# Two-layer encoder step on one core: FFN norm by single tiles, scalars and rows of ones moved, RWKV state chain begun earlier

## What is computed

```python
def _layer(x, past, mem_k, mem_v, l, mw, ow):
    y, new_state = _mixer_sublayer(_rmsnorm(x, norm_mix_pre), past, l, mw)
    x = x + _rmsnorm(y, norm_mix_post)
    x = x + _rmsnorm(_cross_attention(_rmsnorm(x, norm_x_pre), mem_k, mem_v, w_xq, w_xo), norm_x_post)
    x = x + _rmsnorm(_swiglu(_rmsnorm(x, norm_ffn_pre), w_ffn_in, w_ffn_out), norm_ffn_post)
...
    # in the mixer: one projection for all three branches
    a_q, a_k, a_v, a_f, b_q, b_k, b_v, c_in, gate_in = _split_cols(h @ w_in, IN_SPLITS)
    # the scalar of differential attention
    lam = jnp.exp(jnp.sum(lq1 * lk1)) - jnp.exp(jnp.sum(lq2 * lk2)) + lam_init
...
def step(S, xs):  # RWKV-7, frame by frame
    rt, wt, kt, vt, kkt, at = xs
    sa = jnp.einsum('bhvk,bhk->bhv', S, -kkt)
    S = S * wt[:, :, None, :] + sa[..., None] * (kkt * at)[:, :, None, :] + vt[..., None] * kt[:, :, None, :]
    return S, jnp.einsum('bhvk,bhk->bhv', S, rt)
```

## Time and profile before

| what | value |
|---|---|
| runs | 3005.76, 3007.36, 15319.49 us; median 3007.36 us |
| profiled execution | 3008.48 us, its span 3006.7 us |
| TensorE busy | 2861.5 us, 95% |
| weight loads of TensorE | 2644.9 us, 88% |
| VectorE busy | 1637.3 us, 54% |
| ScalarE busy | 746.2 us, 25% |
| transfers | 290.26 MB, 97 GB/s on average |
| chain that ended last | 81% TensorE, 9% VectorE, 3% ScalarE, 2% transfers |

### The profile page before, as it was taken

The page is one execution under the profiler, slowest core; times in us unless marked ns, Lnnn a source line. Parts: engine busy times, 40 slices in busy tenths (PEclk is TensorE's granted clock), DMA queues, the critical chain, the costliest instruction groups (busy, mean ns, idle before and its releaser), DMA issues.

```text
span 3006.7 us, 63127 instructions
## 1 busy us (share of the span) xinstructions
PE 2861.5 (95%) x26468; PEld 2644.9 (88%) x26468; DVE 1637.3 (54%) x3027; ACT 746.2 (25%) x1789; POOL 243.6 (8%) x423
## 2 busy tenths in 40 slices
PE   7999999999999989999989999999999999899998
PEld 6877788999999789999988777799999997899998
DVE  4444554666674356664364445546666633566633
ACT  1133333323233330000112333342222323200001
POOL 1111111000000100000001211120000000000000
PEclk9999999999999999999989998899999999999999
DMA  4443345222163223332224434362222531233331
GB/s 123 125 131 99 98 130 138 83 79 73 39 185 98 60 80 89 87 88 86 78 78 134 114 96 121 98 161 72 78 62 65 175 98 43 85 88 88 87 86 62
DMA packets 420762, 290.26 MB, mean 97 GB/s; under 512 B 38544, under 2 KB 386352, under 8 KB 420352
## 3 DMA queue, kind: packets, MB, share of 16 engines
q1 hardware_dynamic: 398496, 228.64, 27.3%
q0 software_dynamic: 21984, 57.59, 6.0%
HBM read 232.12 MB, written 54.07 MB: 95 GB/s over the span
## 4 chain that ended last, share of the span: by engine, by line
PE 81%; DVE 9%; ACT 3%; DVEq 3%; issue 2%; DMA 2%; ACTq 0%; SPq 0%
PE PS L714 33%; PE PS L781 10%; PE PS L1077 7%; PE PS L1019 7%; PE PS L692 4%; PE PS L946 2%; PE PS L1226 2%; DMA U<-gate_scratch 2%; ACT U L1333 1%; PE PS L657 1%; PE PS L1056 1%; PE PS L863 1%; PE PS L828 1%; ACT U L1336 1%; PE PS L730 1%
## 5 line engine op out<-in xcount | busy, mean ns | idle before, releaser
L714 PE MATMUL PS<-U_r,WHI 128*128 128x272 f32 x2656 | 475.4, 290 | 18.0 <-DVEq L1833 9.2
L1336 ACT COPY U<-PS 128x272 f32<-128x272 f32 (+9 forms) x756 | 263.3, 372 | 752.4 <-PE PS L1077 140.0
L1822 DVE CAST WHI<-ring 128x1024 fp32r<-128x1024 f32 (+1 forms) x240 | 164.2, 684 | 512.4 <-PE PS L714 379.2
L714 PEld LDWEIGHTS PS<-U_r,WHI 128*128 128x128 f32 x2656 | 387.2, 189 | 23.3 <-DVEq L2250 10.8
L714 PE MATMUL PS<-brT_r,WHI 128*128 128x272 f32 x1728 | 357.5, 288 | 0.0
L714 PE MATMUL PS<-U_r,WLO 128*128 128x272 f32 x1696 | 351.2, 289 | 0.0
L714 PE MATMUL PS<-hT_r,WHI 128*128 128x272 f32 x1696 | 351.1, 289 | 0.0
L1832 DVE TENSOR_TENSOR WLO<-ring,WHI 128x1024 fp32r<-128x1024 f32 (+1 forms) x240 | 289.8, 1208 | 19.0 <-issue 0.9
L781 PE MATMUL PS<-U_r,WHI 128*128 128x272 f32 x832 | 268.2, 322 | 15.8 <-ACT U L1336 15.7
L714 PE MATMUL PS<-brT_r,WLO 128*128 128x272 f32 x1344 | 278.2, 288 | 0.0
L714 PEld LDWEIGHTS PS<-brT_r,WHI 128*128 128x128 f32 x1728 | 271.7, 188 | 0.2
(11 more groups left out here) (328 smaller groups left out, 4470.6 us busy)
## 6 DMA issues: line engine op xcount, KB each, us to landing
ring<-in_w_in_dram SPq DMA_DIRECT2D x126, 512.0 KB, 4.2
ring<-in_w_ffn_in_dram SPq DMA_DIRECT2D x88, 512.0 KB, 3.8
ring<-in_w_ffn_out_dram SPq DMA_DIRECT2D x32, 448.0 KB, 3.7
proj_scratch<-U POOLq DMA_DIRECT2D x104, 136.0 KB, 2.0
U<-proj_scratch SPq DMA_DIRECT2D x48, 272.0 KB, 4.4
ring<-in_w_branch_dram SPq DMA_DIRECT2D x48, 256.0 KB, 3.3
gate_scratch<-U POOLq DMA_DIRECT2D x88, 136.0 KB, 3.1
U<-gate_scratch SPq DMA_DIRECT2D x44, 272.0 KB, 2.9
```

The costliest lines, as they stand in the source:

```text
L714: ins = mm(PS[:, 2 * q + h, 0:HT], w, half(x, h), start=(first and k == 0 and n == 0), stop=(last and k == kn - 1 and n == len(terms) - 1))
L1336: return act.copy(out, in_)
L1822: copy(hi, src)
```

## The change

- FFN norm: x is updated, split and multiplied one tile at a time, not two. VectorE's `updated(b)` scales and adds one tile, `low(b)` follows with one tile and its own `x_split`; ScalarE makes one high part and one square in turn; TensorE takes 12 matmuls of one input tile, then its 4 sum matmuls. `X_SPLITS` counts eight signals in place of four.
- Input projection: the lambda scalars, ScalarE's exponential between them and the rows of ones move behind the split and copy of the second output tile (v = 1).
- RWKV: the turn of the sample's starting state moves on TensorE from behind stage 10 to behind the second sum ahead of the stages, its copy on VectorE ahead of stage 1. VectorE evacuates only group 0 of stage 10 before the chain; groups 1 and 2 come behind the first and the second decay multiply, and `rw_free` behind them.
- Forgetting attention: the second weight split of a pass moves from step 8 to step 9.

```diff
@@ -52,7 +52,7 @@
-X_SPLITS = 4 + 6 + 4
+X_SPLITS = 4 + 6 + 8
...
@@ -719,10 +719,11 @@
 
                 pe.wait_ge(split_done, l * SPLITS + v + 1 + 2)
                 freed(l, g + 1)
-                for k0 in range(0, KM, 2):
-                    pe.wait_ge(x_split, l * X_SPLITS + need + k0 // 2 + 1)
+                step = 2 if sums is None else 1
+                for k0 in range(0, KM, step):
+                    pe.wait_ge(x_split, l * X_SPLITS + need + k0 // step + 1)
                     for j in range(2):
-                        for k in (k0, k0 + 1):
+                        for k in range(k0, k0 + step):
                             whi, wlo = (w[:, (v + j) % 2, k, :] for w in (WHI, WLO))
                             xhi, xlo = rhs(k)
                             for n, (w, x) in enumerate(((whi, xhi), (whi, xlo), (wlo, xhi))):
@@ -732,8 +733,7 @@
                         if k == KM - 1:
                             ins.then_inc(tile_done, 1)
                     if sums is not None:
-                        for a in (k0, k0 + 1):
-                            norm_sum(l, sums, a)
+                        norm_sum(l, sums, k0)
...
@@ -1065,6 +1065,11 @@
                         gate(q0 + 1, 1, it=it)
                         pe.wait_ge(rw_in, g * 2 + 2)
                         sums(W_RAW[:, 2, :]).then_inc(rw_sum, 1)
+                        halves = (slice(0, 64), slice(64, 128))
+                        eye = const("stack")[:, 0:64]
+                        for r in halves:
+                            ins = mm(PS[r, 5, 256:320], ST[r, 11, :], eye[r], start=True, stop=True)
+                        ins.then_inc(rw_state, 1)
                         both(q0 + 2, it)
...
@@ -1146,11 +1151,6 @@
-                        halves = (slice(0, 64), slice(64, 128))
-                        eye = const("stack")[:, 0:64]
-                        for r in halves:
-                            ins = mm(PS[r, 5, 256:320], ST[r, 11, :], eye[r], start=True, stop=True)
-                        ins.then_inc(rw_state, 1)
                         for c in range(9):
...
@@ -1385,9 +1385,6 @@
-                act.wait_ge(lam_step, l * 2 + 1)
-                f(small[:, 14:16], small[:, 12:14], ACT.Exp)
-                act.drain().then_inc(lam_step, 1)
...
@@ -1404,6 +1401,10 @@
                     tile(l, G_IN + v)
                     copy(half(EST[:, e % 4, :], 0), PS[:, 2 * IN_PAIR[v], 0:HT]).then_inc(tile_freed_act, 1)
+                    if v == 1:
+                        act.wait_ge(lam_step, l * 2 + 1)
+                        f(small[:, 14:16], small[:, 12:14], ACT.Exp)
+                        act.drain().then_inc(lam_step, 1)
                     e += 1
...
@@ -1715,12 +1716,10 @@
-                for a in range(0, KM, 2):
-                    for b in (a, a + 1):
-                        act.wait_ge(x_updated, l * 24 + 16 + b + 1)
-                        f(HF[:, b, :], xT[:, b, :], ACT.Copy, scale=vec("norm_ffn_pre", b)).then_inc(h_ready, 1)
-                    for b in (a, a + 1):
-                        norm_square(l, 4, b)
+                for b in range(KM):
+                    act.wait_ge(x_updated, l * 24 + 16 + b + 1)
+                    f(HF[:, b, :], xT[:, b, :], ACT.Copy, scale=vec("norm_ffn_pre", b)).then_inc(h_ready, 1)
+                    norm_square(l, 4, b)
                 norm_rstd(l, 4, RSF)
...
@@ -1849,24 +1848,6 @@
-                dve.wait_ge(vec_loaded, (l + 1) * 16 * 19)
-                tt(lamp[:, :, :], lam4[:, 0:4:2, :], lam4[:, 1:4:2, :], ALU.mult)
-                dve.drain()
-                dve.tensor_reduce(small[:, 12:14], lamp[:, :, :], AX.X, ALU.add)
-                dve.drain().then_inc(lam_step, 1)
-                dve.wait_ge(lam_step, l * 2 + 2)
-                c0 = _c["lam"][0]
-                tt(small[:, 16:17], small[:, 15:16], small[:, 14:15], ALU.subtract)
-                dve.drain()
-                tt(small[:, 16:17], small[:, 16:17], CB[:, ds(l + c0, 1)], ALU.subtract)
-                tt(small[:, 17:18], vec("diff_subln", 0), CB[:, ds(l + (c0 + 2), 1)], ALU.mult)
-                dve.drain()
-                dve.memset(FQ[0][64:66, :, :], 1.0)
-                dve.memset(FK[0][64:66, :, :], 1.0)
-                dve.memset(ONES, 1.0)
-                dve.drain().then_inc(fx_rows, 1)
...
@@ -1881,6 +1862,23 @@
+                    if v == 1:
+                        dve.wait_ge(vec_loaded, (l + 1) * 16 * 19)
+                        tt(lamp[:, :, :], lam4[:, 0:4:2, :], lam4[:, 1:4:2, :], ALU.mult)
+                        dve.drain()
+                        dve.tensor_reduce(small[:, 12:14], lamp[:, :, :], AX.X, ALU.add)
+                        dve.drain().then_inc(lam_step, 1)
+                        dve.wait_ge(lam_step, l * 2 + 2)
...
+                        dve.drain()
+                        dve.memset(FQ[0][64:66, :, :], 1.0)
+                        dve.memset(FK[0][64:66, :, :], 1.0)
+                        dve.memset(ONES, 1.0)
+                        dve.drain().then_inc(fx_rows, 1)
...
@@ -1948,8 +1946,8 @@
-                        if k in (3, 8):
-                            late_split(3 * it + k // 8)
+                        if k in (3, 9):
+                            late_split(3 * it + k // 9)
...
@@ -2144,6 +2142,8 @@
+                        dve.wait_ge(rw_state, g * 10 + 1)
+                        copy(ST[:, 8, :], PS[:, 5, 256:320]).then_inc(rw_chain, 1)
                         dve.drain()
                         for gr in range(3):
                             dve.sem_inc(rw_ev[gr], 1)
...
@@ -2199,18 +2199,19 @@
-                        for s in range(1, 11):
+                        for s in range(1, 10):
                             for gr in range(3):
                                 evac(s, gr)
-
-                        dve.wait_ge(rw_state, g * 10 + 1)
-                        copy(ST[:, 8, :], PS[:, 5, 256:320]).then_inc(rw_chain, 1)
-                        dve.drain().then_inc(rw_free, 1)
+                        evac(10, 0)
                         for c in range(9):
                             dve.wait_ge(rw_state, g * 10 + c + 2)
                             to = c + 1 if c < 7 else c + 2
                             ts(ST[:, to, :], PS[:, 2 * (c // 3) + c % 3 % 2, 0:CHUNK], DCOL[:, c:c + 1], None, ALU.mult) \
                                 .then_inc(rw_chain, 1)
+                            if c < 2:
+                                evac(10, c + 1)
+                            if c == 1:
+                                dve.drain().then_inc(rw_free, 1)
                             if c % 3 == 2:
                                 evac(11, c // 3)
                         dve.sem_inc(rp_y, 1)
...
@@ -2326,28 +2327,23 @@
-                def scaled(a):
-                    for b in (a, a + 1):
-                        stt(hT[:, b, :], hT[:, b, :], vec("norm_x_post", b), RS, ALU.mult, ALU.mult)
+                def updated(b):
+                    stt(hT[:, b, :], hT[:, b, :], vec("norm_x_post", b), RS, ALU.mult, ALU.mult)
                     dve.drain()
-
-                def added(a):
-                    for b in (a, a + 1):
-                        tt(xT[:, b, :], xT[:, b, :], hT[:, b, :], ALU.add).then_inc(x_updated, 1)
-
-                def low(a):
-                    for b in (a, a + 1):
-                        dve.wait_ge(h_ready, l * 24 + 16 + b + 1)
-                        stt(hTR[:, b, :], xT[:, b, :], vec("norm_ffn_pre", b), HF[:, b, :].bitcast(F32), ALU.mult, ALU.subtract)
+                    tt(xT[:, b, :], xT[:, b, :], hT[:, b, :], ALU.add).then_inc(x_updated, 1)
+
+                def low(b):
+                    dve.wait_ge(h_ready, l * 24 + 16 + b + 1)
+                    stt(hTR[:, b, :], xT[:, b, :], vec("norm_ffn_pre", b), HF[:, b, :].bitcast(F32), ALU.mult, ALU.subtract)
                     dve.drain().then_inc(x_split, 1)
 
-                scaled(0)
-                added(0)
-                for a in range(2, KM, 2):
-                    scaled(a)
-                    low(a - 2)
-                    added(a)
+                updated(0)
+                updated(1)
+                for b in range(2, KM):
+                    low(b - 2)
+                    updated(b)
                 low(KM - 2)
+                low(KM - 1)
                 dve.wait_ge(xa_stored, (l + 1) * 32)
```

More of the change, by code:

```diff
@@ L1883, in _ @@
                     e += 1
+                    if v == 1:
[5 more added lines that the diff above has]
+                        dve.wait_ge(lam_step, l * 2 + 2)
+                        c0 = _c["lam"][0]
+                        tt(small[:, 16:17], small[:, 15:16], small[:, 14:15], ALU.subtract)
+                        dve.drain()
+                        tt(small[:, 16:17], small[:, 16:17], CB[:, ds(l + c0, 1)], ALU.subtract)
+                        tt(small[:, 17:18], vec("diff_subln", 0), CB[:, ds(l + (c0 + 2), 1)], ALU.mult)
+                        dve.drain()
```

(4 more changed lines are left out.)

## The result

The changed kernel took 2967.3 us, the median of four executions, against 3009.2 us for the kernel before, also four in the same series. That is 42 us less, where 26.6 were forecast, and 8 us under the range of 2975 to 2990. One execution of each kernel was a slow one (6009.5 and 15319.5 us); over the other three the medians are 2962.6 (2959.4 to 2972.0) and 3007.4 us, 45 us apart, with a ratio of 0.9853, 95% interval 0.9827 to 0.9878. Two later series of the same changed kernel gave 2981.1 and 2981.0 us.

The account below looks back on a forecast made before the run. TensorE was taken to bound the kernel. Terms 12.8 (scalars) + 0.9 (FFN) + 6.2 (RWKV) + 6.7 (forgetting attention) = 26.6 us, so 3008.5 - 26.6 = 2981.9 us; range 2975 to 2990.

Parts of the forecast that it names:

- scalars: holes: Input projection: third tile's weight split no longer waits behind scalars and rows of ones; TensorE starts 4.07 and 3.76 us sooner, 7.8.
- scalars: clock behind the hole: Input projection: the 112 matmuls behind the shortened hole run at full clock, 2.33 + 2.70 = 5.0 us saved; other bound 0.
- FFN norm: FFN norm by single tiles: first matmul 2.02 us sooner, 0.46 left per layer, 0.9 in all; bounds 4.0 to -4.6.
- RWKV, eight passes: RWKV state chain: third product's last term 0.89 us sooner, less 0.12, 0.77 x 8 = 6.2 us; bounds 0 and 8.5.
- split in the forgetting attention: Forgetting attention: weight split moved a step later ends TensorE's 1.12 us hole in six passes, 6.7 us; bounds 0 and 7.4.
- The first rival: Input projection: the short hole behind the second tile keeps the half clock, 5.0 us not had, 2986.9 us; chance 0.08.
- the wait before the third tile: FFN norm: TensorE waits about 0.8 us before the third FFN tile, whose weights are split when tile 0 is done.
- the return to the norm's sums: FFN norm: sums interleaved eight times, not four; each return costs TensorE 0.20 us, four more of them 0.8.
- the 0.12 for the moved turning matmuls: RWKV: the 4 turning matmuls, moved into a stretch that TensorE bounds, cost 576.52 - 576.40 = 0.12 us.
- RWKV gives nothing: RWKV: evacuations between the first steps hold the chain as before, kernel at 2988.1 us; chance 0.10.

Follow-up runs that it names:

- the four filled runs: 12 weight-split matmuls moved between sample transposes and values in differential attention: kernel before 2981.2 us; changed kernel 2958.1, 2960.1, and 2957.5 with ten extra norm-sum matmuls.
- the filled changed kernel: Changed kernel with 12 weight-split matmuls moved between the differential attention's 32-wide sample transposes and values: 2958.1 us, then 2960.1 against 2981.0 unaltered.

## Why the prediction was wrong

Term by term, in the two profiled executions:

| step | forecast | measured |
|---|---|---|
| scalars: holes | 7.8 | 3.74 + 3.89 = 7.6 |
| scalars: clock behind the hole | 5.0 | 2.06 + 2.43 = 4.5 |
| FFN norm | 0.9 | 0.47 + 0.62 = 1.1 |
| RWKV, eight passes | 6.2 | 8 x 0.47 = 3.8 |
| split in the forgetting attention | 6.7 | 3.7 + 0.8 = 4.5 |
| differential attention | none | 13.8 + 10.7 = 24.5 |
| all else | none | -0.2 |

**The scalars: right.** In the first layer the hole went to 1.02 and not to 0.7, since from the split's start to TensorE's it took longer than the 2.08 forecast: 50.67 - 48.18 = 2.49. In the second layer it was 2.07 and the hole 0.60. The first rival, that a short hole keeps the half clock, fell: clock 1.00 in the window that begins with the third tile. The rule of the Trainium skill that was weighed (TensorE: Matmul & The Clock Gate, section A second HAM failure mode: psum-queue depth-cycling) speaks of frequent micro-idles, and this was one isolated hole: the clock stayed at 1.00 behind it, and 4.5 of the 5.0 us came.

**The FFN norm: right in mechanism and in size.** The first tile came 2.1 us sooner relative to the norm (forecast 2.02) and the wait before the third tile is 0.51 (forecast about 0.8). The term that was a little too dear is the return to the norm's sums: a tile with its sums takes TensorE 2.42 us at full clock (sums at 1071.98, 1074.41 and 1076.82), where 2.52 were forecast.

**RWKV: one term mis-sized.** The chain gained what was forecast: from its first product to the last term of the third 555.25 - 553.53 = 1.72 us, against 2.66 before, 0.94 for a forecast of 0.89. What failed is the 0.12 for the moved turning matmuls. It was read off the start times of one engine where they stood behind 64-wide work of their kind. Between the sums (L1056) and the stages they stand between 128-wide matmuls. TensorE's timeline from the sums to the first stage, of before and then of after:

```profile
609.44 1.13 PE L1056 MATMUL PS<-U,CB 128*128 128x288 f32 x4
...
616.54 4.49 PE L1077 MATMUL PS<-U 64*64 64x128 f32 x84
```
```profile
585.63 1.13 PE L1056 MATMUL PS<-U,CB 128*128 128x288 f32 x4
586.70 0.33 PE L1071 MATMUL PS<-CB,U 64*64 64x64 f32 x4
...
593.16 4.50 PE L1082 MATMUL PS<-U 64*64 64x128 f32 x84
```

616.54 - 609.44 = 7.10 became 593.16 - 585.63 = 7.53. They cost 0.43 (0.43 to 0.47 in the eight passes), 3.5 times the forecast, and 0.94 - 0.43 is the 0.5 of a pass. The rival "RWKV gives nothing" is wrong too.

**The weight split: right, and given back.** Six passes are 1.18 shorter each, 7.1 us, a little over the 6.7. But the second layer's first pass is 2.8 us longer, at half clock (window of after):

```profile
1583.40:1590.20 6.80, 6.38 (x27) 5.98 (x27) 1.07 (x4) 1.69 (x6) 3.15 (x5) 0.50 0.28 78
```

**The step that failed** is none of the four. The sum took the clock of every stage that the change doesn't touch as given: a term put at nothing without a reason, which measured 24.5 us in the differential attention of the two profiled executions. The prediction asked "does this hole still cost the clock?" in one place, and its range of 15 us had no term for the clock anywhere else. Yet the profiled kernel before spends 127 us of its span at half clock, worth 63 us, which is more than the whole change; the changed one spends 69. Over all 13 executions of the changed kernel: full-clock time 2925.8 on average, 17.9 under before, against 26.6 - 5.0 = 21.6 forecast. Of the 3.7 missing some 2 are the way that a hole in half-clock time counts (an estimate from where the half clock lies in the trace of before); RWKV's 2.4 less and what the FFN and the split gave more make up the rest. Half-clock time is 59 to 119 and on average 99, some 30 less than before, worth 15 us, where the forecast had 5. So the change saves about 33 us on average, 18 of work and waiting and 15 of clock, and 23 to 50 against the average of before in a given execution. That the median of the 13, 2980.0, is near the 2981.9 forecast is partly luck, two errors that cancel: 3.7 us too much from the work, 10 too little from the clock.

**What is shown and what is not.** Shown: the time that the sum missed is half-clock time in stages that the change leaves as they were. A delay of 0.9 to 2.7 us in an unchanged kernel moves its time by -18 to +6 us, through half-clock time. With 12 matmuls put into the thin stretch both kernels have less half-clock time in their own series, 75 for 125 and 67 for 108 us. Supported but not shown: that the thin stretch is what makes the clock fall. For it, the half-clock time is only 41 to 84 us in every execution of the four filled runs, of both kernels. Against it as the only cause, filling shifts the later work too, a delay alone did as much once, and the first layer's first pass still fell in all three traces of the filled changed kernel. Not shown: why the change lowers the half-clock time on average. It shifts the first attention by 10 us and the second by 33, and nothing here says that another 33 would have done as well; the delays say rather that they might not. Also open is what differs between two executions of one kernel, one of which has the half clock in an attention and the other not.

## What to carry to other kernels

When a kernel's mean clock is under 1.00, work out what the clock costs, span x (1 - clock), before the sum of any change. If that is more than the change is worth, a mere shift may outweigh the change with either sign, as the delays of -18 to +6 us did here, and the range has to hold that. Run both kernels in more than one series: one trace is one draw. Look for thin stretches on TensorE, a hole beside narrow matmuls, in a loop that is otherwise dense: moving dense work into one, from behind it, took 26 us off the kernel before, where the four planned steps took 18 in full-clock time. And price a moved group of matmuls where it lands, by the neighbours that it will have.

## What was not expected of the hardware

- The clock fell behind a hole of only 0.54 us with 32-wide matmuls around it, and in other traces behind one of 0.76 us with narrow work ahead of it, but not in every pass that has them; it didn't fall behind lone holes of 1.02 and 1.12 us between 128-wide work.
- Once fallen in one head pass, it tends to fall in the next, at the same point of the code: passes take 41.1 us at 1.00, 42.6 at 0.96, 44.1 at 0.92 and 47.3 at 0.86, and in the trace of before all eight passes have some half clock.
- The same kernel on the same chip spreads over 12 to 17 us, and span x clock takes about half of that out: in the last series of before, full-clock times lie within 2939 and 2947, each known to 1.5 us, while the times go from 3000.6 to 3017.3.
- Two products of 64 x 64 (four instructions) put between 128-wide matmuls cost 0.43 us; where they stood behind 64-wide work, the next product started only 0.12 us after their own start.
